# A routed-expert block in float32 on one core: every expert matrix brought in by two transfers of 2 MB, the first place refilled in quarters, and the adding of an expert's rows moved

## What is computed

```python
for e in range(N_EXPERTS):                      # 32
    g = jnp.minimum(t @ w_gate[e] + b_gate[e], SWIGLU_LIMIT)
    u = jnp.clip(t @ w_up[e] + b_up[e], -SWIGLU_LIMIT, SWIGLU_LIMIT)
    act = (u + 1.0) * (g * jax.nn.sigmoid(SWIGLU_ALPHA * g))
    out = out + comb[:, e:e + 1] * (act @ w_down[e] + b_down[e])
```

## Time and profile before

| | us |
|---|---|
| median of 3 runs | 1089.0 (1088.84 to 1089.39) |
| the profiled execution's own time | 1089.41 |
| its span, first to last instruction | 1087.6 |
| PE busy | 1040.9 (96%) |
| DVE, ACT, POOL busy | 269.2, 189.3, 29.5 |
| read from HBM | 431.61 MB, 398 GB/s over the span |
| granted TensorE clock | 0.996 of full |

### The profile page before, as it was taken

The page is one execution under the profiler, slowest core; times in us unless marked ns, Lnnn a source line. Parts: engine busy times, 40 slices in busy tenths (PEclk is TensorE's granted clock), DMA queues, the critical chain, the costliest instruction groups (busy, mean ns, idle before and its releaser), DMA issues.

```text
span 1087.6 us, 12106 instructions
## 1 busy us (share of the span) xinstructions
PE 1040.9 (96%) x5078; PEld 445.1 (41%) x5078; DVE 269.2 (25%) x552; ACT 189.3 (17%) x342; POOL 29.5 (3%) x41
## 2 busy tenths in 40 slices
PE   9999999999999999999999998999999999999997
PEld 5889984333333333333333332333333333333332
DVE  6876563111111111111111111111111111111111
ACT  4656623000010000100001000010000000000001
POOL 0070020000000000000000000000000000000000
PEclk9999999999999999999999999999999999999999
DMA  9834997999999999999999999999999999999996
GB/s 306 308 112 163 352 411 317 377 433 433 428 434 429 424 437 430 424 431 429 430 433 429 431 438 429 425 436 430 422 434 434 427 431 427 427 428 428 426 426 260
DMA packets 37227, 433.12 MB, mean 398 GB/s; under 512 B 5157, under 2 KB 5706, under 8 KB 18762
## 3 DMA queue, kind: packets, MB, share of 16 engines
q1 hardware_dynamic: 36704, 432.11, 94.6%
q10 hardware_dynamic: 490, 0.56, 0.2%
HBM read 431.61 MB, written 1.05 MB: 398 GB/s over the span
## 4 chain that ended last, share of the span: by engine, by line
PE 51%; DMA 39%; DVE 7%; ACT 2%; issue 1%; SPq 0%; DVEq 0%; ACTq 0%
PE ps L909 36%; DMA ring<-in_exp_w_up 22%; DMA arena<-in_exp_w_gate 4%; DMA arena<-in_exp_w_down 4%; DMA ring<-in_exp_w_gate 4%; DMA arena<-in_exp_w_up 4%; PE ps L881 3%; PE ps L611 2%; PE ps L613 2%; PE ps L612 2%; PE ps L875 2%; DVE ring_r L1361 2%; DVE arena L1634 2%; DMA ring<-in_w_in 1%; DVE arena L1632 1%; ACT ring_r L1047 1%
## 5 line engine op out<-in xcount | busy, mean ns | idle before, releaser
L909 PE MATMUL ps<-ring,arena 128*64 128x512 f32 x2432 | 541.6, 597 | 22.2 <-DMA ring<-in_exp_w_gate 13.4
L909 PEld LDWEIGHTS ps<-ring,arena 128*64 128x64 f32 x2432 | 168.0, 137 | 348.0 <-issue 309.9
L909 PE MATMUL ps<-arena 128*64 128x512 f32 x640 | 143.7, 601 | 8.3 <-DMA arena<-in_exp_w_gate 6.9
L1620 DVE TENSOR_SCALAR arena<-ps 128x512 f32<-128x512 f32 x30 | 20.7, 691 | 430.1 <-PE ps L909 430.1
L909 PEld LDWEIGHTS ps<-arena 128*64 128x64 f32 x640 | 45.3, 138 | 94.9 <-issue 83.7
L1632 DVE TENSOR_SCALAR arena<-ps 128x512 f32<-128x512 f32 x32 | 22.1, 692 | 241.3 <-PE ps L909 241.3
L1214 ACT COPY arena<-ps 128x512 f32<-128x512 f32 x30 | 17.6, 586 | 302.4 <-PE ps L869 302.4
L881 PE MATMUL ps<-arena 64*128 64x512 f32 x264 | 65.9, 616 | 1.6 <-issue 0.9
L1212 ACT ACTIVATE arena<-arena 128x512 f32<-128x512 f32 x30 | 18.9, 629 | 241.3 <-DVE arena L1620 241.3
L869 PE MATMUL ps<-arena 128*64 128x512 f32 x256 | 60.4, 592 | 0.0
L611 PE MATMUL ps<-ring_r 128*128 128x256 f32 (+1 forms) x192 | 59.4, 309 | 1.0 <-ACT arena L1072 0.6
(11 more groups left out here) (218 smaller groups left out, 632.3 us busy)
## 6 DMA issues: line engine op xcount, KB each, us to landing
ring<-in_exp_w_down SPq DMA_DIRECT2D x49, 2048.0 KB, 40.1
ring<-in_exp_w_up SPq DMA_DIRECT2D x22, 4096.0 KB, 36.5
ring<-in_exp_w_gate SPq DMA_DIRECT2D x16, 4096.0 KB, 38.0
ring<-in_exp_w_gate SPq DMA_DIRECT2D x18, 2048.0 KB, 40.2
arena<-in_exp_w_down SPq DMA_DIRECT2D x13, 2048.0 KB, 40.1
arena<-in_exp_w_gate SPq DMA_DIRECT2D x6, 4096.0 KB, 35.9
arena<-in_exp_w_up SPq DMA_DIRECT2D x5, 4096.0 KB, 36.5
ring<-in_exp_w_up SPq DMA_DIRECT2D x8, 2048.0 KB, 44.1
```

Of the source, the lines that this page charges most:

```text
L909: last = mm(ps[BLOCK * to:BLOCK * (to + 1), bank, :], src[:, c, half, :], hold_chunks(at)[:, half, c, HALF * to:HALF * (to + 1)], start=(f ...
L1620: v.tensor_scalar(g1, ps[:, 4, :], LIMIT, None, ALU.min).then_inc(g_ready, 1)
```

## The change

- `halved(n)` is true for all 96 matrices: each comes in two transfers of 2 MB (the further cuts of `TAIL` stay).
- The first matrix that comes back to a used place (n = 5, down of expert 1, place 0) has its first half cut in two: 1 MB when PE has used the first quarter of gate 0 (`gate_quarter`), 1 MB when it has used the half. The first of them signals `quarter_in`, for which ACT waits ahead of its load of `rounds`.
- The rows of expert i are added behind the down product of expert i + 1, in place of between its gate and its up product; `turn_weights(5)` follows them there. ACT copies `pickT` behind its wait for the down product. Rows of expert 29 are still added between gate 30 and up 30.
- The last expert's rows are added within `last_pair`, ahead of the branch. The counts of `scattered` for which ACT and DVE wait become `rounds * 4 + ...`, since the four products that put the residual into the banks now count too.

```diff
         def halved(n):
-            return matrix(n)[1] == 2 or n % PASS == 6 or n >= MATRICES * FINE
+            return 0 <= n < MATRICES * E
...
-                if not at_start:
-                    first_half, both_halves = 2 * (n - HOLDS) + 1, 2 * (n - HOLDS) + 2
+                first_back = isinstance(r, int) and isinstance(base, int) and n == HOLDS
+                first_half, both_halves = 2 * (n - HOLDS) + 1, 2 * (n - HOLDS) + 2
+                if first_back:
+                    sp.wait_ge(gate_quarter, 1)
+                elif not at_start:
                     sp.wait_ge(piece_done, of_round + (first_half if halved(n) else both_halves))
...
-                sp.dma_start(hold(k)[:, 0, :], src[:, 0, :]).then_inc(matrix_in[k], 16)
+                if first_back:
+                    sp.dma_start(hold(k)[:, 0, 0:2 * D], src[:, 0, 0:2 * D]).then_inc(quarter_in, 16)
+                    sp.wait_ge(piece_done, 1)
+                    sp.dma_start(hold(k)[:, 0, 2 * D:], src[:, 0, 2 * D:]).then_inc(matrix_in[k], 16)
+                else:
+                    sp.dma_start(hold(k)[:, 0, :], src[:, 0, :]).then_inc(matrix_in[k], 16)
...
             def start_from_residual(t, half):
-                mm(ps[:, 2 * t + half, :], ident, xt[:, t, HALF * half:HALF * (half + 1)], start=True, stop=True)
+                mm(ps[:, 2 * t + half, :], ident, xt[:, t, HALF * half:HALF * (half + 1)],
+                   start=True, stop=True).then_inc(scattered, 1)
...
+                        if quarter_signal and half == 0 and c == 1:
+                            last.then_inc(quarter_signal, 1)
...
-                product(r, step, n, 4, h_in)
+                product(r, step, n, 4, h_in, quarter_signal=gate_quarter)
                 pe.wait_ge(y_ready, i + 1)
                 pe.wait_ge(pickT_ready, i + 1)
-                scatter(y_e, pickT)
+                if n == GATE30:
+                    scatter(y_e, pickT)
                 biases(1, 5, next_e)
...
                 turn(7, act_out).then_inc(act_T, 1)
-                turn_weights(5)
                 pe.wait_ge(hg_ready, i + 2)
                 turn(6, h_got).then_inc(h_turned, 1)
...
                 product(r, step, MATRICES * j + 2, 7, actT, fresh=True)
+                scatter(y_e, pickT)
+                turn_weights(5)
...
                 scatter_tile(1, y_e, pickT).then_inc(rows_down, 1)
+                pe.wait_ge(pickT_ready, i + 3)
+                pe.wait_ge(y_ready, i + 3)
+                scatter(last_y, last_pickT, signal=scattered)
...
-            pe.wait_ge(pickT_ready, rounds * E + 1)
-            pe.wait_ge(y_ready, rounds * E + 1)
-            scatter(last_y, last_pickT, signal=scattered)
...
+            act.wait_ge(quarter_in, 16)
             act.wait_ge(rounds_ready, 1)
...
+                act.wait_ge(piece_done, done * PIECES_PER_EXPERT + (PIECES_PER_EXPERT * j + 6))
                 act.wait_ge(pick_T, done + (j + 1))
                 nc.scalar.copy(pickT, ps[:, 5, 0:S]).then_inc(pickT_ready, 1)
-                act.wait_ge(piece_done, done * PIECES_PER_EXPERT + (PIECES_PER_EXPERT * j + 6))
                 nc.scalar.copy(y_e, ps[:, 7, :]).then_inc(y_ready, 1)
...
-                act.wait_ge(scattered, 2 * t + 1)
+                act.wait_ge(scattered, rounds * (2 * NT) + (2 * t + 1))
...
-                dve.wait_ge(scattered, 2 * t + 2)
+                dve.wait_ge(scattered, rounds * (2 * NT) + (2 * t + 2))
```

More of the change, by code:

```diff
@@ L354, in build @@
         weights_ready = sem("weights_ready")
+        gate_quarter = sem("gate_quarter")
+        quarter_in = sem("quarter_in")
         rows_down = sem("rows_down")
@@ L889, in scatter, with product @@
                     scatter_tile(t, y, weights, signal)
-            def product(r, step, n, bank, src, between=None, fresh=False):
+            def product(r, step, n, bank, src, between=None, fresh=False, quarter_signal=None):
                 at = n % HOLDS
@@ L1009, in _ @@
                 with pe.Fori(1, rounds) as r:
-                    pe.wait_ge(pickT_ready, r * E + 1)
-                    pe.wait_ge(y_ready, r * E + 1)
-                    scatter(last_y, last_pickT)
                     pe.wait_ge(pick_ready, r * E + 1)
```

## The result

The changed kernel takes 1091.27 us (median; 1089.81 to 1092.18), the kernel before 1089.19 us (1088.82 to 1089.69), 16 runs of each. The ratio is 1.0018, with an interval of 1.0012 to 1.0025: the change makes the kernel slower by 2.1 us, where I had forecast 0.4 us less. The profiled execution has a time of 1091.77 us and a granted clock of 0.999 of full, against 0.996 before, so TensorE's clock plays no part.

What follows compares the result with a forecast made beforehand. The DMA engines were taken to bound the kernel; +4.9 (halves) - 4.4 (two holes) - 0.9 (tail) = -0.4 us gave 1089.0 for the profiled execution, 1088.6 us for the median. Range 1084.5 to 1092.7, likeliest 1086.5 to 1091.8.

Steps and rivals of the forecast that it cites:

- What bounds the kernel: Whole run: DMA engines set the end, 29.3 us an expert against PE's 27.1, plus a tail on PE and writes.
- Part 1: Start of the experts: first used place refilled in quarters, first issue moves from 180.74 to about 178.97; gain 1.77 us.
- no stretch under 400 GB/s between 185 and 230: Sign expected in the DMA profile after the change, between 185 and 230 us, if the second hole closes.
- Part 2: Second DMA hole, 202.00 to 206.50 us, closes: gain 2.6 us; with Part 1 4.4, bounds 3.7 to 5.0.
- Part 3: Expert stream: 45 matrices in halves with 16 KB rows, 0.128 us more each; 4.9 us loss taken, bounds 2.2 to 10.4.
- The value with the code given back: Stretch behind 930 us: removing the 0.3% taken by code pages makes the loss from halves 3.5 us; 4.9 was taken.
- A microsecond in which they stand still, or move less, is a microsecond of the whole time.: Whole run: time the DMA engines lose anywhere was counted one for one at the end.
- Part 5: Tail: last scatter ahead of the branch starts 0.9 us earlier, with copies and writes; gain 0.9 us, bounds 0 to 1.0.
- Part 4: Experts: moved work on PE and ACT makes PE's expert 27.5 us, still under 29.3; costs nothing.
- The one on the slower side: Expert stream: halves move slower than in the sum, at 425 GB/s costing 9 us; total 1092.7; chance 0.17.
- The size of a transfer costs nothing: Expert stream: lower rate behind 930 us has other causes, halves cost 0 to 1 us; total 1084.6; chance 0.20.
- The branch only changes hands: Tail: moving the last rows ahead of the branch gives nothing; total 1089.5; chance 0.2 within the likeliest case.

Runs made afterwards that it cites:

- without_quarter: The changed kernel with the first half of n = 5 again in one 2 MB transfer; 1090.68 us, ratio 1.0015 to the kernel before.
- move_halves: The changed kernel without the 1 MB quarters and with the last expert's rows back behind the branch; 1089.57 us, ratio 1.0003 to the kernel before.
- move_alone: The kernel before with only scatter and turn_weights moved behind the down product, ACT's lines exchanged to match; 1087.90 us, ratio 0.9988.
- after_again: The changed kernel itself, unaltered, run once more on the same chip as its variants; 1091.11 us, ratio 1.0016 to the kernel before.
- levelled: The changed kernel with SP waiting ahead of n = 75 until n = 74 has landed, so the queue runs dry once; 1093.68 us, ratio 1.0043.
- dve_free: The changed kernel without DVE's wait for down 31 ahead of its branch; 1089.25 us, ratio 1.0000 to the kernel before.
- tail_alone: The kernel before with only the last expert's rows put ahead of the branch; 1090.20 us, ratio 1.0009.
- without_tail: The changed kernel with the last expert's rows back behind the branch; 1089.83 us, ratio 1.0004 to the kernel before.
- sparse: The changed kernel with gate and up whole (4 MB) again except each pass's third gate and third up and all from n = 81; 1088.39 us, ratio 0.9996.
- sparse_dve_free: sparse, also without DVE's wait for down 31 ahead of its branch; 1088.28 us, ratio 0.9992 to the kernel before.
- sparse9_dve_free: sparse_dve_free with the fourth gate of each pass (n % 15 == 9) in halves too; 1088.63 us, ratio 0.9993 to the kernel before.

## Why the prediction was wrong

**What bounds the kernel** was right: every kernel's end goes back to the landing of down 31.

**Part 1** (1.77 us): the issue at 179.09 came as worked out, and the 1.8 us were there at 27.5 MB. The step "The slow first packets come 1.77 us earlier, too, and aren't saved" failed. With the early start a second group of slow packets followed at 186 to 191 us, which before doesn't have in that form (a few lie at 192.7 to 194.8), and about 0.35 us remained. With it failed the sign "no stretch under 400 GB/s between 185 and 230": 184.50 to 192.00 has 389. The runs show that starting early brings these packets, not why they are slow.

**Part 2** (2.6 us): right in mechanism, and the issues came at 198.56 (forecast 198.4) and 208.10 (208.3). By the engines' mean it gave 3.3 us (without_quarter at 41 MB). Together the two parts gave 3.7 (at 41 MB) and 3.5 (at 50 MB), at the lower bound of 3.7 for the 4.4.

**Part 3** (4.9 us): right in mechanism, wrong in size. The lead of 3.5 us at 50 MB shrinks to 0.23 at 408 MB: 3.3 us, within the bounds. For 45 matrices that is 0.07 us each where I had taken 0.128 and then 4.9 us for all. Without quarter and tail it is the same: move_halves goes from 3.0 us ahead to 0.2 behind, while move_alone, without the halves, keeps its 1.5. By rate it shows as well: 428 GB/s from 230 to 910 us and 427 behind, so part of the lower rate behind 930 us was that stretch's own and not the size. The value with the code given back, 3.5, was the nearer one, and I had set it aside.

The three terms give the mean 0.2 us of gain, where the sum had 4.9 - 4.4 = 0.5 us of loss. So the terms that I sized weren't what turned the sign. Two steps did:

**The 16 engines were taken for one.** The step is "A microsecond in which they stand still, or move less, is a microsecond of the whole time." Parts 1 to 3 count bytes over all engines and put the difference at the end of the run. Down 31 starts when the last engine has landed its share. In after the last is 3.20 us behind the eighth, before 1.57. The transfer for which down 31 waits shows it directly: the mean of its 16 landings is 1069.92 in after and 1070.15 before, 0.23 earlier, but the last one is 1073.38 against 1072.17, 1.21 later, and the product follows it by 0.14. So down 31 starts 1.20 us later although the bytes are 0.2 us ahead. In after_again it is 0.63 us. Why the engines drift apart, by more in one kernel than in another, is open. The prediction's bounds for what closing a hole is worth (3.7 to 5.0) left this out. That an idle queue lets the engines draw level, as levelled shows, makes the last hole worth less than its length.

**Part 5** (0.9 us gain, bounds 0 to 1.0). The `scatter` came 1.05 us earlier, and ACT's first copy 1.13, as said. The lower bound rested on "ACT or DVE, which pass the same branch, aren't back in time for the copies": that happened for DVE, by 1.2 us (+3.21 against +1.99 in dve_free). Zero was no bound, because I hadn't asked what PE's branch, moved behind the `scatter`, would now fall beside. Its page of code falls among the writes. So the term was a loss in place of 0.9 us of gain: 1.16 us in the profiled executions, in the medians 1.0 (tail_alone) to 1.4 (after against without_tail).

**Part 4** (nothing) was right. The chain of after at the start of the experts, as the earlier trace rows:

```profile
177.18 7.02 PE ps L920 x32
...
201.96 1.92 PE ps L892 x8
203.87 0.37 PE ps L934 x2
...
204.48 7.02 PE ps L920 x32
```

From gate 0 to gate 1 PE needs 27.3 us (27.5 forecast), under the 29.3 of the DMA engines, and the next gate follows at 231.84.

**The rivals.** The one on the slower side had the wrong mechanism: the halves were cheaper than in the sum, not dearer. "The size of a transfer costs nothing" is refuted by sparse against after (2.9 us). "The branch only changes hands" was the nearest to what came, and it stopped at zero. The case that happened, engines apart and a branch that falls among the writes, was none of mine. The time lies within the range of 1084.5 to 1092.7, but for other reasons than those the range was made of.

## What to carry to other kernels

When a queue feeds 16 engines, count the last engine, not the mean: look at how far the shares of one transfer land apart before and after, and don't count on a filled hole to pay all its bytes (here 1.5 us of a closed hole paid 1.3, and a pause of 4.1 us cost 2.4). Before work is put ahead of a branch, look at every engine that has the same branch, and at what its fetch of code will then lie beside. Try splitting only those transfers whose issue waits for PE; here one more halved matrix in fifteen, with the moved rows, gave 2.1 us, and halving all of them gave it back.

## What the runs showed of the hardware that I had not expected

- DVE's branch at the end held it for 3.0 us. PE's branch instruction lasts 3.86 us in after (from 0.83 to 4.69 us behind the end of down 31, the last `scatter` running beside it), while ACT's next instruction came 0.5 us behind its branch.
- A 16 KB page of code among the writes took 0.96 us in after (0.88 to 1.24 among the late pages of all kernels). The last engine's writes stood still meanwhile, and the first three 2 KB packets behind it took 189 to 231 ns in place of 85.
- Packets of 16 KB took 0.9 to 2.3 us in place of 0.61 some 7 to 12 us after an early restart of the queue, in all ten profiled executions with that start, and not when the same transfers were issued 1.7 us later. Why is open.
- In a full queue a matrix of 4 MB in two transfers costs about 0.07 us more than in one (3.3 us for 45).
- The 16 engines drift apart in a full queue: the last share of a transfer lands 0.95 to 3.20 us behind the eighth, by kernel.
- The time outside the span is 1.8 to 1.9 us in most runs here, and 2.5 to 3.3 us in all runs of sparse_dve_free and sparse9_dve_free. Why is open.
